# FoX value projection in token-major form: tokens as the stationary factor and 512 weight columns moving, in place of four projections and their transposes

## What is computed

```python
u = _rmsnorm(h, g_pre[i])                     # (1040, 1024)
qa, ka, va, za, qf, kf, vf, zf, ff, ga, gf = jnp.split(u @ w_in[i], split_idx, axis=-1)
log_f = jax.nn.log_sigmoid((ff + b_forget[i]).astype(jnp.float32))
y_fox = _fox_branch(qf..., kf..., vf..., log_f) * jax.nn.silu(zf)
#   logits = q k^T * scale + (c_i - c_j), c = cumsum(log_f); causal softmax; probs @ v
merged = sigmoid(ga + b) * (y_swa @ w_up_swa[i]) + sigmoid(gf + b) * (y_fox @ w_up_fox[i])
h = h + _rmsnorm(merged @ w_out[i], g_post[i])
```

## Time and profile before

| | |
|---|---|
| median of three runs | 819.14 us (818.04 to 823.6) |
| the profiled execution | 819.36 us, span 817.5 us |
| TensorE busy | 97% of the span, 4462 matmuls |
| weight loads busy | 79% |
| DVE, ScalarE, GpSimd busy | 61%, 39%, 41% |
| DMA | 116 MB, mean 142 GB/s |
| TensorE idle between the end of the `vs` entry and the first product (66.10 to 154.1 us) | 0.75 us |

### The profile page before, as it was taken

One profiled execution on the slowest core, in us unless ns is written; L12 is line 12 of the kernel. 1 busy time (PEld: TensorE's weight loads), 2 busy tenths in 40 slices (PEclk: granted clock), 3 DMA queues, 4 the chain that ended last, 5 costly groups with the idle time before them and its releaser, 6 DMA issues.

```text
span 817.5 us, 12789 instructions
## 1 busy us (share of the span) xinstructions
PE 792.9 (97%) x4462; PEld 648.6 (79%) x4462; DVE 497.9 (61%) x1065; ACT 316.1 (39%) x649; POOL 337.9 (41%) x287
## 2 busy tenths in 40 slices
PE   6999999999999999999999999999998999999997
PEld 4999999988888888888888866756664788878885
DVE  6845788366777877745746466676778744442222
ACT  6532241333334333333333337666677122231111
POOL 1112213454535535444445325747785244412221
PEclk9999999999999999999999999999999999999999
DMA  9342424459845335344344599999900565352222
GB/s 277 107 127 56 131 66 120 125 163 232 216 135 158 113 90 147 103 122 120 97 133 121 139 243 238 228 229 224 229 2 2 203 182 155 103 206 77 103 78 77
DMA packets 120185, 116.08 MB, mean 142 GB/s; under 512 B 29741, under 2 KB 92029, under 8 KB 120122
## 3 DMA queue, kind: packets, MB, share of 16 engines
q1 hardware_dynamic: 118824, 111.53, 51.2%
q10 hardware_dynamic: 1298, 3.74, 1.2%
HBM read 81.99 MB, written 34.96 MB: 143 GB/s over the span
## 4 chain that ended last, share of the span: by engine, by line
PE 80%; issue 6%; POOL 5%; DVE 4%; ACT 3%; DMA 2%; SPq 0%; DVEq 0%; ACTq 0%; POOLq 0%
PE PS L1896 20%; PE PS L1897 20%; PE PS L1898 20%; PE PS L2158 4%; PE PS L2160 4%; PE PS L2159 4%; POOL acc L1242 3%; PE PS L2019 2%; DVE t_val L1631 2%; DMA QBs<-q_dram 2%; PE PS L2081 1%; POOL w_plain L1194 1%; PE PS L1928 1%; ACT p_fox L1399 1%; PE PS L2096 1%
## 5 line engine op out<-in xcount | busy, mean ns | idle before, releaser
L1173 POOL TENSOR_TENSOR ops<-s_sum,ops 128x512 fp32r<-128x512 f32 x64 | 89.1, 1402 | 106.6 <-ACT ops L1271 106.6
L1896 PE MATMUL PS<-t_hi,ops 128*128 128x512 f32 x256 | 100.3, 392 | 0.0
L1898 PE MATMUL PS<-t_hi,ops 128*128 128x512 f32 x256 | 100.0, 391 | 0.0
L1897 PE MATMUL PS<-t_lo,ops 128*128 128x512 f32 x256 | 100.0, 391 | 0.0
L1173 POOL TENSOR_TENSOR ops<-raw,ops 128x512 fp32r<-128x512 f32 x48 | 65.8, 1372 | 64.4 <-ACT ops L1271 64.0
L1194 POOL TENSOR_TENSOR w_plain<-raw,w_plain 128x1024 fp32r<-128x1024 f32 x10 | 27.7, 2768 | 100.7 <-ACT w_plain L1300 100.7
L1242 POOL TENSOR_TENSOR acc<-acc,p_fox 128x400 f32<-128x400 f32 (+5 forms) x76 | 59.9, 808 | 5.0 <-ACT p_fox L1399 4.0
L1713 DVE TENSOR_TENSOR z_tmp<-u,PS 128x512 f32<-128x512 f32 x48 | 33.0, 686 | 45.7 <-PE PS L1898 26.5
L1271 ACT ACTIVATE ops<-s_sum 128x512 fp32r<-128x512 f32 x64 | 39.6, 624 | 52.6 <-DVE s_sum L1507 46.8
L1399 ACT ACTIVATE p_fox<-PS,neg_c_col 128x512 f32<-128x512 f32 (+5 forms) x112 | 54.3, 536 | 13.8 <-PE PS L2067 9.2
L1898 PEld LDWEIGHTS PS<-t_hi,ops 128*128 128x128 f32 x256 | 48.2, 188 | 10.2
(11 more groups left out here) (212 smaller groups left out, 2144.5 us busy)
## 6 DMA issues: line engine op xcount, KB each, us to landing
raw<-in_w_in_dram SPq DMA_DIRECT2D x34, 512.0 KB, 5.2
q_dram<-stage_b SPq DMA_DIRECT2D x32, 256.0 KB, 2.4
g_dram<-stage_b SPq DMA_DIRECT2D x32, 256.0 KB, 2.0
tanh_g<-g_dram SPq DMA_DIRECT2D x16, 512.0 KB, 3.9
x_all<-in_x_dram SPq DMA_DIRECT2D x8, 512.0 KB, 7.2
raw<-in_w_in_dram SPq DMA_DIRECT2D x16, 256.0 KB, 4.6
z_dram<-stage_b SPq DMA_DIRECT2D x16, 256.0 KB, 2.0
QAs<-q_dram SPq DMA_DIRECT2D x16, 256.0 KB, 7.9
```

The costliest lines, as they stand in the source:

```text
L1173: nc.gpsimd.tensor_tensor(ops[:, i % OPS, 1], op_source(p, name), ops[:, i % OPS, 0].bitcast(F32), ALU.subtract).then_inc(op_ready, 1)
L1896: pe.matmul(dst, hi_w, hi, start=first, stop=False)
L1897: pe.matmul(dst, hi_w, lo, start=False, stop=False)
L1898: return pe.matmul(dst, lo_w, hi, start=False, stop=last)
```

## The change

The four entries `vf` are no longer projected and transposed. Their weights are split into two new tiles `wv` (high and low, 8 k-tiles x 512 columns), and a new step `tokens` makes for each tile of 128 tokens one bank of 128 x 512: the tokens of `u` are the stationary factor, and the 512 columns of all four blocks move. ScalarE or DVE copies the bank to one slot of `stage_a`, and SP stores it with one DMA. The 16 meta rows come last: `u_meta` holds their high rows twice and their low rows at column 32, so that one matmul of 48 stationary columns gives high x high and low x high in different partitions, and DVE adds the two; a second of 16 columns gives high x low.

The order of the stage changes with it. `PLAIN` puts the four `vf` entries ahead of `kf1` to `kf3`; their weights are split after the chunks of `vs`, one per chunk; the nine token steps follow, with the transposes of `vs` after the second and the forget gate's `columns` after the third; and then the last three key entries. The sums of `u` begin at the fourth token step. The places of sums 1 and 3 in memory are those of `wv`, so these two begin when the token steps are done. `wv` lies where the rows of x were, so the first split waits for the last transpose of x. The forget gate's cumulative sum now overwrites `f_ones`, and the x rows for the last stage share three semaphores.

```diff
-PLAIN = [("f", 0), ("ks", 0), ("kf", 0), ("vs", 0), ("vf", 0), ("kf", 1), ("vf", 1), ("kf", 2), ("vf", 2), ("vf", 3),
+PLAIN = [("f", 0), ("ks", 0), ("kf", 0), ("vs", 0), ("vf", 0), ("vf", 1), ("vf", 2), ("vf", 3), ("kf", 1), ("kf", 2),
          ("kf", 3)]
+FIRST_VF, LATE_KF = 4, 8
+V_LOW = 32
...
+            ("hi", 2), ("lo", 0), ("val", 1, 0), ("val", 1, 1), ("hi", 1), ("lo", 2), ("val", 3, 0), ("val", 3, 1),
+            ("hi", 3), ("lo", 1), ("lo", 3)]
...
+    for c in range(4):
+        ch = chunk(3, c)
+        steps.append(ch)
+        steps.append(drain(ch))
+        steps.append(dict(kind="split_w", entry=FIRST_VF + c))
+        if c == 0:
+            steps.append(dict(kind="meta_rows"))
+        if c < 2:
+            steps.append(dict(kind="forget", t=c))
+    for n in range(NQ + 1):
+        who = ("act", "dve")[count["group"] % 2] if n < NQ else "dve"
...
+        if n == 1:
+            steps.append(values(3))
+        if n == 2:
+            count["dve"] += 1
+            steps.append(dict(kind="columns", g=count["group"], who="dve", n=count["dve"]))
...
+        if n == 4:
+            steps.append(dict(kind="split_w", entry=LATE_KF))
+        if n >= 3:
+            sum_step(1)
+    for e in range(LATE_KF, len(PLAIN)):
         for c in range(4):
             ch = chunk(e, c)
             steps.append(ch)
-            if c == 1 and PLAIN[e - 1][0] in ("vs", "vf"):
-                steps.append(values(e - 1))
             steps.append(drain(ch))
             if c == 1 and e + 1 < len(PLAIN):
                 steps.append(dict(kind="split_w", entry=e + 1))
-            if e == 3 and c < 2:
-                steps.append(dict(kind="forget", t=c))
...
+            sum_step(1)
...
+        token_sum(0)
+        value_weights(0)
+        token_sum(1)
+        token_sum(2)
+        value_weights(1)
+        token_sum(3)
...
+                    elif PLAIN[e][0] == "vf":
+                        cols = slice(P * PLAIN[e][1], P * (PLAIN[e][1] + 1))
+                        nc.gpsimd.tensor_tensor(wv[1][:, :, cols], raw[:, s], wv[0][:, :, cols].bitcast(F32),
                                                 ALU.subtract).then_inc(w_ready, 1)
...
+                    if e >= LATE_KF:
+                        act.wait_ge(chunk_done, last_chunk[{0: 2, 1: 3, 2: 1}[plain_slot(e)]] + 1)
+                    elif e == FIRST_VF:
+                        act.wait_ge(u_transposed, 2 * NK)
...
+                elif kind == "tokens":
+                    n, g = st["n"], st["g"]
+                    t0, r = token_rows(n)
+                    free_bank_of(g)
+                    if n == 0:
+                        pe.wait_ge(w_ready, FIRST_VF + PAIRS)
+                    elif n == NQ:
+                        pe.wait_ge(meta_rows, 3)
+                    dst = PS[:, g % V_RING, :]
+                    for k in range(KT):
+                        if n < NQ:
+                            ins = three(dst, u_part(False, k, t0, r), u_part(True, k, t0, r), wv[0][:, k, :],
+                                        wv[1][:, k, :], k == 0, k == KT - 1)
+                            continue
...
+                        ins = pe.matmul(dst[0:V_LOW + N_META], u_meta[:, k, :], wv[0][:, k, :], start=k == 0,
+                                        stop=k == KT - 1)
+                    ins.then_inc(transposed, 1)
```

More of the change, by code:

```diff
@@ L146, in plain_steps, with sum_step @@
     sums = [("val", 0, 0), ("val", 0, 1), ("val", 0, 2), ("hi", 0), ("val", 2, 0), ("val", 2, 1), ("val", 2, 2),
[L147 to L150, removed]
+            ("hi", 2), ("lo", 0), ("val", 1, 0), ("val", 1, 1), ("hi", 1), ("lo", 2), ("val", 3, 0), ("val", 3, 1),
+            ("hi", 3), ("lo", 1), ("lo", 3)]
+    def sum_step(n):
+        for _ in range(n):
+            if sums:
+                x = sums.pop(0)
+                steps.append(dict(kind="t_" + x[0], t=x[1], x=x[2] if x[0] == "val" else 0))
+                if sums and sums[0][0] == "hi":
+                    x = sums.pop(0)
+                    steps.append(dict(kind="t_hi", t=x[1], x=0))
+    for c in range(4):
[9 more added lines that the diff above has]
+        who = ("act", "dve")[count["group"] % 2] if n < NQ else "dve"
+        count[who] += 1
+        steps.append(dict(kind="tokens", n=n, g=count["group"], who=who, done=count[who], use=count["stage"]))
+        count["group"] += 1
+        count["stage"] += 1
+        if n == 1:
[3 more added lines that the diff above has]
+            steps.append(dict(kind="columns", g=count["group"], who="dve", n=count["dve"]))
+            count["group"] += 1
+        if n == 4:
[3 more added lines that the diff above has]
+    for e in range(LATE_KF, len(PLAIN)):
         for c in range(4):
@@ L412, in build @@
         uB1_lo = sb("uB1_lo", [P, HK, BANK], F32R, on=early)
+        f_x = sb("f_x", [HEADS, LENGTH], on=early)
+        f_e = sb("f_e", [HEADS, LENGTH], on=early)
+        f_ones = sb("f_ones", [HEADS, LENGTH], on=early)
+        neg_c_rows = f_ones
         x_all = sb("x_all", [P, NQ + 1, D_MODEL], on=early)
@@ L811, in build @@
         columns_freed = next(st["n"] for st in steps_a if st["kind"] == "columns")
[L812 to L819, removed]
-            elif st["kind"] == "columns":
-                groups = st["g"] + 1
         turns = {i + 2: st["head"] // 2 for i, sts in maxima.items() for st in sts if st["final"] and st["head"] % 2}
@@ L838, in build, with token_rows @@
                         acc_before[n] = acc_free[n - 2]
+        def token_rows(n):
+            return (0, N_META) if n == NQ else (N_META + n * P, P)
         def stage_a_free(engine, n):
@@ L1571, in _ @@
                     else:
-                        done = sum(1 for g in group_owner if g < values_before[ch["entry"]])
-                        if done:
-                            dve.wait_ge(transposed, done)
                         nc.vector.tensor_copy(v_t[:, tok], src).then_inc(chunk_drained, 1)
```

84 lines of the change are left out of this document (64 added, 20 removed).

## The result

The changed kernel took 830.78 us (four runs, 829.38 to 831.47) against 818.86 of the kernel before on the same chip: ratio 1.0128, 95% interval 1.0095 to 1.016. It is slower, by more than the 824.4 us forecast and outside its range of 819.0 to 829.0.

The account below looks back on a forecast made before the run. TensorE, with a matmul in flight for 97% of the span, was taken as the bound. 819.36 - 2.9 (matmuls) + 4.8 (first wait) + 1.6 (clock) + 1.5 (key entries) = 824.4 us; range 819.0 to 829.0.

Parts of the forecast that it names:

- the wait for kf3: Last key entries: TensorE waits 0.8 to 2.8 us for kf3's split weights; +1.5 us taken, bounds 0 and 4.5.
- the first wait: First token tile: TensorE waits for four vf weight splits instead of one, restarting near 71.46 instead of 66.66; +4.8 us.
- the far end of +7: Upper bound of the first token tile's delay, if one later GpSimd subtraction takes 4.49 us; lower bound +4.6.
- matmuls and transposes: Value projection on TensorE: four vf entries and their transposes leave, 208 matmuls of 512 columns come; -2.9 us.
- GpSimd's three subtractions: Low halves before the first token tile: vf1 64.12 to 66.61, vf2 and vf3 2.4 us each, to 71.4.
- clock behind it: After the first token tile's wait: clock falls, 3.4 us of slow matmuls at about half work; +1.6 us, 0 to 3.2.
- the dearer of the two prices: 512-column matmuls start 0.226 or 0.235 us apart; 0.228 taken for wv, the dearer price as rival giving 825.9 us.
- clock stays up: Rival at the first token tile: 5.4 us of idleness does not lower the clock; 822.8 us, chance 0.28.
- Key entries: kf1 to kf3: late sums delay a key drain, its staging slot and kf3's weight split behind it; +1.5 us.
- The rival in which DVE becomes the bound: In kf1 and kf2, key drains and sums fill DVE's queue; 5 to 8 us instead of 1.5, 828 to 831, chance 0.14.
- Slower by over 1%: Outcome above 827.3 us: nearly all of the DVE case and the upper end of the first forecast; chance 0.15.

Follow-up runs that it names:

- experiments 1: Changed kernel with all four vf weight splits ahead of the forget gate's exp and ln on every queue: 820.74 us, ratio 1.0008.
- experiment 3: Changed kernel, forget gate's second DVE part behind token tile 0: 830.9 us (first); also waiting for all four low halves: 826.49 us (held).
- experiment 5: Changed kernel with ten filling matmuls ahead of TensorE's wait for kf3's weights: 829.09 us, ratio 1.0114.
- experiment 2: Changed kernel with filling matmuls on the identity ahead of the wait for the vf weights: 834.76 us with 68, 828.01 us with 34.
- 6: Changed kernel with the four vf splits ahead of the forget gate and the kf2 and kf3 splits in the token stage: 816.45 us, ratio 0.9968.

## Why the prediction was wrong

Two steps failed, one term that was too small and one that was not there. Either alone leaves the sum inside the range of 819.0 to 829.0; with both, and the 1.0 us by which the wait for kf3 passed my +1.5, it is at 829.6, close to the profiled execution (829.38); the median of 830.78 lies beyond.

**The term that was too small** is the first wait, +4.8 where +7.6 was measured. It rests on one sentence: "vf1 64.12 to 66.61 as in the row, then vf2 and vf3 at 2.4 us each". I took the 2.49 us of the earlier trace rows for a subtraction that ran beside DVE's scan and was not hurt, and carried it on. The row was read without its neighbour. In the kernel before, the scan that began at 64.39 is listed with 4.39 us:

```profile
64.39 4.39 DVE L1605 TENSOR_TENSOR_SCAN neg_c_rows<-f_ones,f_x 8x1040 f32<-8x1040 f32 x1
68.82 0.69 DVE L1608 CAST f_e<-neg_c_rows 8x1040 fp32r<-8x1040 f32 x1
```

Alone it takes 2.31 (experiments 1 and 3): it was the scan that stood still, and once there was a second and a third subtraction, they and DVE's next instructions took turns. I had that price in the bounds, by the 4.49 us of the earlier trace rows, and put it at the far end of +7, which the measured +7.6 passes; over the 6.98 us of three subtractions alone the measured 9.55 are 2.6 more, one turn of 2.0 and a part of another.

**The term that was not there** is the clock behind the wait for kf3: the sum has +1.5 for the wait and nothing for what follows, and the runs showed +1.6 behind it (experiment 5 takes it away).

Term by term, against the kernel before:

| step | forecast | measured | from |
|---|---|---|---|
| matmuls and transposes | -2.9 | -2.93 | 151.00 less 66.46, before 154.13 less 66.66 |
| first wv matmul later | +4.8 | +7.56 | 74.22, 66.66 |
| in it, GpSimd's three subtractions | 7.3 | 9.55 | its rows; alone 6.98 |
| clock behind it | +1.6 | +1.46 | table above, experiment 2 |
| wait for kf3's weights | +1.5 (0.8 to 2.8) | +2.52 | gap ahead of 151.11 |
| clock behind that | not in the sum | +1.59 | table above, experiment 5 |
| sum | +5.0 | +10.20 | first product +10.18 |

- **Matmuls: right.** Tiles whose stationary tokens are from `uA` go at 0.232 us a matmul, those from `uB` at 0.227, the meta rows at 0.230. In the second stage, where they move, `uA` goes at 0.233 and `uB` at 0.229. So the dearer of the two prices of the earlier trace rows goes with `uA` being read, in whichever role, and `wv` does not decide it, as I had taken; why `uA` is dearer is open. The mean, 0.229 for my 0.228, was right by luck of the halves.
- **First wait: mechanism and place right, size wrong**, as above. ScalarE's split came at 63.41 (63.0 forecast); 0.4 us of the start is exp's later place, 60.05 in place of 59.64 of the earlier trace rows.
- **Clock behind it: mechanism right, size partly by luck.** It cost 1.5 us here and 2.6 to 2.8 in the four other profiles with an idle wait at this place, after 5.5 to 8.5 us without work. The +1.6 met the shorter stretch; the bound of 3.2 holds all five. The eight records until 16.95 in the earlier trace rows that I read as eight matmuls of 0.21 us are four (`FILL` in the kernel), two records each as in experiment 2: 0.42 us a matmul against 0.218 there, so slow they were. The rival "clock stays up" fell.
- **Key entries: the chain was right**, slot by slot, at the upper part of the 0.8 to 2.8, because GpSimd's subtraction stood for one turn of DVE. The 4.03 us of the earlier trace rows came back at two sums (4.17 and 3.97). The rival in which DVE becomes the bound did not occur: one wait, not over 2.5 us, behind ScalarE's drain and not behind DVE.
- **The second fall was missed.** I had asked what TensorE does after 5.4 us of idleness, and not after 2.5; the only fall that the earlier trace rows shows came 3.9 us after the last matmul, which seemed to clear short waits. The fall came in the profile of the changed kernel and in those of experiments 1, 2 (both) and 3 (first), and not in that of experiment 3 (held).
- **Chances.** "Slower by over 1%" had 0.15. The 5.2 us that are missing are 2.8 at the first wait, 1.0 at kf3 and 1.6 of the second fall, less 0.1 at the clock: nearly all to one side. I had taken the first wait near the lower end of its bounds and the second in the middle, and the range did not add the two: +7 at the first wait and 2.8 at kf3 together would have given 827.9, and with the second fall 829.5.

The change itself is good for 2.9 us, and two orders of steps decide whether they are seen: with the splits ahead of the forget gate and the key splits in the token stage the kernel is 0.15 to 0.49% faster than before.

## What to carry to other kernels

When a change makes TensorE wait for several outputs of GpSimd, read DVE's timeline over the same microseconds, and take an instruction's cost from a row where the other engine is still; a long row of the one means that the other was served. Here that held for instructions that read only SBUF, not for DVE's copies and drains out of a bank. Price a wait of TensorE together with what the clock does behind it: here 2.5 us of waiting cost 3.9 to 4.1 in five profiles of six, and 7.6 cost 9 to 10.4. Before giving up a change of data flow whose matmul term is right, look for the step that can be issued earlier on an engine with room.

## What was not expected of the hardware

- DVE and GpSimd exclude each other instruction by instruction in this stretch, on eight partitions as well as on 128: the scan of 8 x 1040 went from 2.31 to 4.38 us, a cast from 0.69 to 2.65, a copy of 128 x 16 bf16 from 0.16 to 2.37 (experiments 1 and 6), a subtraction of GpSimd from 2.33 to 4.35. DVE's instructions that read a bank of TensorE's results were not held (0.42 us at 66.26 in experiment 3, held, and at 148.89 in the changed kernel). In each pair the surplus, 2.0 to 2.2 us, is close to the rest of the other's instruction. The Trainium skill (GPSIMD Engine Reference, Key points) says that GpSimd shares its SBUF interfaces with VectorE, with contention for DVE instructions in a two-port mode or with two SBUF inputs. The rows agree, and show the size of it here: the loser waits for the rest of the other's instruction, so that a scan of 2.31 us took 4.38.
- The granted clock fell to 0.50 about 1.4 us after TensorE had resumed work behind a gap of 2.6 us, and stayed there 3.4 us; in one of six profiles with such a gap it did not.
- Behind the same gap of 8.3 us it stayed low for 8 matmuls in one execution and for about 14 in two others; behind gaps of 5.8 and 8.8 us for 13 and 14.
- A matmul of 128 columns in full float32 takes 0.218 us and leaves two records.
